# Two edits to a two-layer transformer kernel: modulation units summed on GpSimd, and a new order of the last expert group

## The reference

```python
cond = silu(c)                                   # (1, 1024)
mod = cond @ w_ada + b_ada                       # w_ada (1024, 6144), 24 MB
sh1, sc1, g1, sh2, sc2, g2 = split(mod, 6)
h = rms_norm(x) * (1 + sc1) + sh1
proj = h @ w_in                                  # hgrn2 branch, window attention, two gates
x = x + g1 * (merged @ w_out)
h2 = rms_norm(x) * (1 + sc2) + sh2
x = x + g2 * moe_ffn(h2, ...)                    # 32 experts, top 4, 12 MB of weights each
# second layer: stick-breaking attention, short convolution, then
y = y + einsum('nef,efd->nd', act, w_down[group])   # 32 experts of width 256, top 2
```

## Time and profile before

| | us |
|---|---|
| median of three runs | 1562.67 (1560.21 to 1562.7) |
| the profiled execution | 1558.39 |
| its span, first to last instruction | 1556.6 |
| prologue | 0 to about 235 |
| first mixture of experts | to about 1151 |
| second layer, mixing | to about 1341 |
| second mixture of experts | to the end |

### The profile page before, as it was taken

One profiled execution on the slowest core, in us unless ns is written; L12 is line 12 of the kernel. 1 busy time (PEld: TensorE's weight loads), 2 busy tenths in 40 slices (PEclk: granted clock), 3 DMA queues, 4 the chain that ended last, 5 costly groups with the idle time before them and its releaser, 6 DMA issues.

```text
span 1556.6 us, 20914 instructions
## 1 busy us (share of the span) xinstructions
PE 1451.0 (93%) x8700; PEld 757.0 (49%) x8700; DVE 602.3 (39%) x920; ACT 342.8 (22%) x395; POOL 22.7 (1%) x36
## 2 busy tenths in 40 slices
PE   5999999999999999998998989999989999997677
PEld 2878985333323333332332333333338999853343
DVE  3786683232213132321322321323247697422111
ACT  3564332010101010100100100101033474321110
POOL 1100100000000000000000000000000000000000
PEclk9999999999999999999999999999999999999889
DMA  9987589999999999999999999999996447999998
GB/s 382 367 324 276 198 353 398 428 429 429 429 428 425 428 429 428 429 428 427 429 428 428 428 427 429 428 427 428 428 403 218 163 163 287 364 385 423 422 422 316
DMA packets 76832, 594.63 MB, mean 382 GB/s; under 512 B 5434, under 2 KB 6688, under 8 KB 37348
## 3 DMA queue, kind: packets, MB, share of 16 engines
q1 hardware_dynamic: 74448, 588.25, 91.6%
q0 software_dynamic: 1792, 4.86, 0.9%
q10 hardware_dynamic: 532, 0.64, 0.1%
HBM read 592.66 MB, written 1.06 MB: 381 GB/s over the span
## 4 chain that ended last, share of the span: by engine, by line
PE 60%; DMA 35%; DVE 4%; issue 1%; ACT 1%; SPq 0%; DVEq 0%; ACTq 0%
PE PS L563 53%; DMA ring<-in_w_up 26%; DMA ring<-in_w_up_e 7%; PE PS L739 3%; DMA ring<-in_w_ada 1%; PE PS L1514 1%; DVE ring_r L361 1%; PE PS L763 1%; DVE arena L838 1%; PE PS L679 1%; ACT ring_r L356 0%; PE PS L1591 0%; DVE arena L2110 0%; DVE ring_r L1996 0%; DVE small L2101 0%
## 5 line engine op out<-in xcount | busy, mean ns | idle before, releaser
L563 PE MATMUL PS<-ring,arena 128*64 128x512 f32 x3020 | 670.7, 596 | 39.4 <-DMA ring<-in_w_up 27.2
L563 PEld LDWEIGHTS PS<-ring,arena 128*64 128x64 f32 x3020 | 212.4, 137 | 460.0 <-issue 400.7
L563 PE MATMUL PS<-arena 128*128 128x128 f32 (+12 forms) x1240 | 228.9, 441 | 3.7 <-ACT arena L559 1.4
L826 DVE TENSOR_SCALAR arena<-PS 128x512 f32<-128x512 f32 x32 | 22.1, 692 | 480.6 <-PE PS L563 480.6
L542 ACT ACTIVATE arena<-arena 128x512 f32<-128x512 f32 x32 | 20.2, 630 | 696.5 <-DVE arena L826 696.5
L563 PE MATMUL PS<-ring_r 128*128 128x256 f32 (+1 forms) x576 | 170.9, 304 | 0.4 <-DVE ring_r L1996 0.4
L563 PEld LDWEIGHTS PS<-arena 64*128 64x128 f32 (+6 forms) x1240 | 108.6, 164 | 121.3 <-issue 114.7
L563 PE MATMUL PS<-hT_r,ring_r 128*128 128x256 f32 x800 | 150.3, 284 | 0.4 <-DVE ring_r L361 0.4
L361 DVE TENSOR_TENSOR ring_r<-ring,ring_r 128x2048 fp32r<-128x2048 f32 x51 | 116.4, 2291 | 34.9 <-ACT ring_r L356 33.8
L563 PEld LDWEIGHTS PS<-hT_r,ring_r 128*128 128x128 f32 x800 | 126.6, 192 | 2.3 <-issue 1.4
L356 ACT ACTIVATE ring_r<-ring 128x2048 fp32r<-128x2048 f32 x51 | 97.2, 1912 | 102.5 <-PE PS L563 98.5
(11 more groups left out here) (382 smaller groups left out, 974.1 us busy)
## 6 DMA issues: line engine op xcount, KB each, us to landing
ring<-in_w_up SPq DMA_DIRECT2D x128, 2048.0 KB, 21.0
ring<-in_w_down SPq DMA_DIRECT2D x59, 2048.0 KB, 18.8
ring<-in_w_in SPq DMA_DIRECT2D x17, 2048.0 KB, 11.5
ring<-in_w_gate_e SPq DMA_DIRECT2D x14, 2048.0 KB, 19.3
ring<-in_w_down_e SPq DMA_DIRECT2D x13, 2048.0 KB, 20.9
ring<-in_w_up_e SPq DMA_DIRECT2D x13, 2048.0 KB, 19.4
ring<-in_w_ada SPq DMA_DIRECT2D x12, 2048.0 KB, 15.8
ring<-in_w_out SPq DMA_DIRECT2D x4, 2048.0 KB, 7.8
```

Of the source, the lines that this page charges most:

```text
L563: return nc.tensor.matmul(o, w, m, start=first, stop=last)
L826: V.tensor_scalar(glu.rearrange("p (kk b q) -> p kk b q", kk=4, b=2), hu[:, :, :, :, 0], 7.0, None, ALU.min)\
```

## The change

In the prologue six of the eight later modulation units (4, 6, 8, 9, 10, 11) are summed first. GpSimd, in place, multiplies each of the unit's two row blocks (128x2048) by its column of `cond` and adds the second to the first. TensorE then multiplies the one sum by a matrix of ones: 4 matmuls in place of 8. A sum starts when its unit has landed; TensorE waits for the sum. In TensorE's stream the units move back: 4 between the two halves of round 2, 6 behind the q and k transposes, beside 7, 8 behind round 5, 9 behind round 6, 10 behind the attention output, 11 behind round 7. The router loads in GpSimd's queue stand between the sums, and three bias loads count to `ffn_params` (so the counts that wait for it grow by three). Two semaphores are joined into `rowsT`.

In the last group the down weights come in twelve pieces: first the even rows of all columns (4 pieces), then the odd rows of the left columns, then of the right ones. TensorE multiplies both halves' even rows, then waits for `last_left`, finishes the left half, scatters its first tile, waits for `last_right`, finishes the right half, and scatters the other three tiles. Of the keep-warm matmuls, the six before the up matmuls become four, and the two before the down matmuls go.

```diff
+        ADA_SUMMED = (4, 6, 8, 9, 10, 11)
...
+        def moe2_scatter_tile(pe, X, it, b, i):
+            pe.wait_ge(S(f"{X}_ye"), 2 * it + b + 1)
+            mm(PS[:, 4 + 2 * b + i, :], swT2[:, i * P:(i + 1) * P], ye2[:, b * 512:(b + 1) * 512], True, True)\
+                .then_inc(S(f"{X}_scat_done" if i else f"{X}_scat_tile"), 1)
...
-                    keep_warm(6, 7)
+                    keep_warm(4, 7)
...
-            if last:
-                keep_warm(2, 7)
             arrived(pe, 4)
             arrived(pe, 5)
-            for b in range(2):
-                if by_columns and b:
-                    pe.wait_ge(S("last_columns"), 64)
-                for kk in range(2):
...
-                if by_columns:
-                    moe2_scatter(pe, X, it, b, True)
+            if by_columns:
+                down(0, 0)
+                down(1, 0)
+                pe.wait_ge(S("last_left"), 64)
+                down(0, 1)
+                moe2_scatter_tile(pe, X, it, 0, 0)
+                pe.wait_ge(S("last_right"), 64)
+                down(1, 1)
+                moe2_scatter_tile(pe, X, it, 0, 1)
+                for i in range(TT):
+                    moe2_scatter_tile(pe, X, it, 1, i)
...
-            for b in range(2):
+            for kk, c, name in ((0, slice(0, 1024), None), (1, slice(0, 512), "last_left"), (1, slice(512, 1024), "last_right")):
                 for i in (4, 5):
                     for o in range(2):
...
+            def ada_sum(n):
+                u, seen = ADA[n], 3 * ADA_SUMMED.index(n)
+                kp = PRE[u][2]
+                w = slots[SLOT_OF[u]].rearrange("p (k n) -> p k n", k=2)
+                wait(pool, loaded(u))
+                for kk in range(2):
+                    k = 2 * kp + kk
+                    nc.gpsimd.tensor_scalar(w[:, kk, :], w[:, kk, :], sm("cond")[:, k:k + 1], None, ALU.mult)\
+                        .then_inc(S("ada_summed"), 1)
+                pool.wait_ge(S("ada_summed"), seen + 2)
+                nc.gpsimd.tensor_tensor(w[:, 0, :], w[:, 0, :], w[:, 1, :], ALU.add).then_inc(S("ada_summed"), 1)
+            pool.wait_ge(S("cond32"), 1)
+            ada_sum(4)
+            small_load(sm("b_r1"), bc(t["b_router"][0]), "ffn_params")
...
+            router_load(0, 0)
+            ada_sum(6)
+            router_load(1, 0)
...
             pool.wait_ge(S("modrow"), 2)
             row_out(1)
+            for n, which, half in ((8, 2, 0), (9, 0, 1), (10, 1, 1), (11, 2, 1)):
+                ada_sum(n)
+                router_load(which, half)
...
-                for kk in range(2):
+                for kk in range(1 if summed else 2):
                     k = 2 * kp + kk
                     for j in range(4):
                         last = nc.tensor.matmul(PS[32 * j:32 * j + 32, 7, :],
-                                                sm("cond32")[:, 32 * k:32 * k + 32], w[:, kk, 512 * j:512 * (j + 1)],
...
+                                                C("ones")[:, 0:32] if summed else sm("cond32")[:, 32 * k:32 * k + 32],
+                                                w[:, kk, 512 * j:512 * (j + 1)],
...
             first_tokens()
-            ada(4)
...
             keep_warm_short(6, 4)
-            split_cols(2)
+            pe.wait_ge(S("consts"), 16)
+            split_cols(2, between=lambda: ada(4))
             ada(5)
-            ada(6)
             split_cols(3)
...
+            ada(6)
             ada(7)
             split_tokens(4)
...
-            pe.wait_ge(S("modrow"), 2)
-            ada(8)
...
             split_tokens(5)
+            pe.wait_ge(S("modrow"), 2)
+            ada(8)
+            split_cols(6)
             ada(9)
-            split_cols(6)
-            ada(10)
...
-            ada(11)
...
+            ada(10)
             pe.wait_ge(S("hg_scores_in"), 1)
...
             split_cols(7)
+            ada(11)
```

More of the change, by code:

```diff
@@ L752, in moe2_pe, with down @@
                 pe.wait_ge(S(f"{X}_xg"), 2 * it + 4)
-            if last:
-                keep_warm(2, 7)
             arrived(pe, 4)
             arrived(pe, 5)
-            for b in range(2):
-                if by_columns and b:
-                    pe.wait_ge(S("last_columns"), 64)
-                for kk in range(2):
[L761 to L766, removed]
-                if by_columns:
-                    moe2_scatter(pe, X, it, b, True)
+            def down(b, kk):
+                for j in range(4):
+                    q = slice(CAP2 * j, CAP2 * (j + 1))
+                    mm_ = nc.tensor.matmul(PS[q, b, :], aT2[:, kk * P + CAP2 * j:kk * P + CAP2 * (j + 1)],
+                                           moe2_dst(where, 4 + j // 2)[:, 2 * (j % 2) + kk, b * 512:(b + 1) * 512],
+                                           start=kk == 0, stop=kk == 1, tile_position=(0, CAP2 * j))
+                if kk:
+                    mm_.then_inc(S(f"{X}_down_done"), 1)
+            if by_columns:
[9 more added lines that the diff above has]
+                    moe2_scatter_tile(pe, X, it, 1, i)
+            else:
+                for b in range(2):
+                    for kk in range(2):
+                        down(b, kk)
             if not by_columns:
@@ L1156, in _ @@
             small_load(at(A2MAP, "gain"), bc(t["norm_ffn_g_2"][0]), "ffn_gain")
-        NSMALLS = 9 * 16
+        NSMALLS = 6 * 16
         lb_rows = t["lower_bound_logits"].rearrange("l (h k) -> (l h) k", k=P)
@@ L1508, in ada @@
                 b, kp = PRE[u][1:]
-                wait(pe, loaded(u))
                 w = slots[SLOT_OF[u]].rearrange("p (k n) -> p k n", k=2)
-                for kk in range(2):
+                summed = n in ADA_SUMMED
+                if summed:
+                    pe.wait_ge(S("ada_summed"), 3 * ADA_SUMMED.index(n) + 3)
+                else:
+                    wait(pe, loaded(u))
+                for kk in range(1 if summed else 2):
                     k = 2 * kp + kk
@@ L1514, in ada @@
                         last = nc.tensor.matmul(PS[32 * j:32 * j + 32, 7, :],
-                                                sm("cond32")[:, 32 * k:32 * k + 32], w[:, kk, 512 * j:512 * (j + 1)],
-                                                start=k == 0, stop=k == KD - 1, tile_position=(0, 32 * j))
+                                                C("ones")[:, 0:32] if summed else sm("cond32")[:, 32 * k:32 * k + 32],
+                                                w[:, kk, 512 * j:512 * (j + 1)],
+                                                start=k == 0, stop=kp == 3 and (summed or kk == 1), tile_position=(0, 32 * j))
                 last.then_inc(S("ada_done"), 1)
@@ L1525, in _ @@
             pe.wait_ge(S("posf"), 1)
-            nc.tensor.transpose(PS[:, 5, 0:2], rows[64:66, :], ident[64:66, 64:66]).then_inc(S("posT"), 1)
+            nc.tensor.transpose(PS[:, 5, 0:2], rows[64:66, :], ident[64:66, 64:66]).then_inc(S("rowsT"), 1)
             transpose_h(pe, "n1")
@@ L1533, in _ @@
                 last = nc.tensor.transpose(PS[:, 4, c * P:(c + 1) * P], modrow[:, 0, c * P:(c + 1) * P], ident)
-            last.then_inc(S("mod1"), 1)
+            last.then_inc(S("rowsT"), 1)
             keep_warm_short(6, 7)
             first_tokens()
-            ada(4)
             pe.wait_ge(S("hT_V"), 1)
@@ L2240, in _ @@
             sig(TV(bdown, bdown, G2[0:NE, :], ALU.mult), "bdown_scaled")
-            v.wait_ge(S("ffn_params"), 16 * 7)
+            v.wait_ge(S("ffn_params"), 16 * 10)
             v.wait_ge(S("row_in"), 64)
@@ L2372, in _ @@
             count["x_ready"] += 1
-            v.wait_ge(S("ffn_params"), 16 * 8)
+            v.wait_ge(S("ffn_params"), 16 * 11)
             ss, rs = sm("ss"), sm("rs")
```

30 lines of the change are left out of this document (13 added, 17 removed).

## The result

The changed kernel takes 1606.72 us (median of four runs, 1602.25 to 1607.9) against 1561.66 us for the kernel before beside it (1560.21 to 1562.7): a ratio of 1.0286, interval 1.0271 to 1.030, 45 us slower. The forecast was 1562.3, its range 1556.5 to 1576.5. The profiled execution took 1606.95 us, its span is 1604.7 us, 48.1 more than before.

The account below looks back on a forecast made before the run. It took VectorE's chain to set the prologue from 85.19 to 113.11, TensorE behind 115.56, and DMA the first mixture, passing prologue changes on whole. Prologue +1.3 and last group -1.7 gave -0.4: 1562.67 to 1562.3 us, range 1556.5 to 1576.5.

Parts of the forecast that it names:

- GpSimd's sums: Prologue: a sum takes 9.0 us (8.3 to 13.7); all are hidden except unit 10's, which stalls TensorE 2.2 us.
- unit 10: Prologue, behind the attention output: its sum is done at 136.6, wanted at 134.4; TensorE stands 2.2 us (1.5 to 6.9).
- a rival with a chance of 0.25: Prologue: GpSimd and VectorE hold each other up over SBUF reads; +16 there, +13.6 in all, 1576 us; chance 0.25.
- Late load of the projection unit: Prologue, ahead of 85 us: `w_in` 4 lands 2.7 us late, putting VectorE's chain at +0.8 us (-1.6 to +1.4).
- Unit 8 leaves the scores: Prologue, between two score groups: moving unit 8 away removes VectorE's 0.72 us wait at 100.27, gaining 0.7 us.
- Units behind 115.56: Prologue, after round 6 starts on TensorE: three units of 0.92 us replace two of 1.85, gaining 1.0 us in full.
- The last group: Kernel's end: the new order saves 2.6 us and the clock costs 0.9, together -1.7 us.
- its term: Last group, final up matmuls: idle after four keep-warm matmuls may lower the clock; 0 to 1.7 us, taken as 0.9.
- the weights: Last group: down weights are loaded by about 1545.4 and wanted at 1546.3, so covered by 0.9 us.
- The gap of 2.7 us: Last group: TensorE's idle time between the four keep-warm matmuls and the last up matmuls.
- a way to be wrong: Last group: a late load in the last eight pieces of down weights makes the last quarter wait.

Follow-up runs that it names:

- e8: The changed kernel with GpSimd's sums for units 10 and 11 alone, TensorE multiplying both row blocks of the other units: 1578.48 us, ratio 1.0112.
- e4: The changed kernel with GpSimd's scalings and addition on 8 of 2048 columns, all waits and orders kept: 1563.08 us, ratio 1.0013.
- e3: The changed kernel without GpSimd's sums, TensorE multiplying both row blocks of all units at the new places: 1570.75 us, ratio 1.0058.
- e5: The changed kernel with eight GpSimd memsets, which write and don't read, in place of each sum: 1577.02 us, ratio 1.0104.
- e7: e4 with five keep-warm matmuls in TensorE's wait between the score groups, where unit 8 stood before: ratio 1.0015.
- e10: e3 with unit 8 back between the score groups, the other units at their new places: 1566.36 us, ratio 1.0037.
- e9: The changed kernel with eleven keep-warm matmuls ahead of unit 10, in TensorE's wait for GpSimd's sum: ratio 1.0256.

## Why the prediction was wrong

**The step that failed** is *GpSimd's sums*. It failed in two ways.

*The length.* I took a scaling at 2.2 us, near the memset, and the addition's 4.55 as the upper bound, since a scaling has one input less. It takes 5.43 us, more than the addition beside it (4.7 to 4.9), so a sum is 16 us, outside the 8.3 to 13.7. Unit 6's sum, which I called hidden, made TensorE wait 5.18 us, which VectorE's lateness covered. In the forecast the length decides unit 10: its load, the last in a late row of loads, landed 13.5 us behind its issue as predicted (144.97 to 158.4), and the wait for the sum is 11.25 us where I had 2.2 and at most 6.9. e8 shows 8.9 for this alone.

*The sharing.* It was a rival with a chance of 0.25, and it is what happened: e4 and e3 against the changed kernel show that 36 to 43 us of the 45 go with GpSimd's time, and the rows show the holds themselves. SBUF — State Buffer in the Trainium skill, under Who interferes with whom, states these cases: two SBUF inputs against a GpSimd that reads, and a TENSOR_SCALAR in a two-port mode against any; reads of PSUM and reductions go free. The trace agrees on the kinds (2.3 to 4.3 us; 5.24 and 9.92; none at 119.44 and at L2141). It also says that the other side blocks for the whole instruction. That the trace doesn't bear out in two ways: beside GpSimd's scalings VectorE's two-input instructions got through with a third of the scaling still to run, and the split at 185.55 wasn't held at all; in e5 the hold ran over several memsets in a row, 10 us of 14. I argued from the absence of a row, where nothing spoke against the rule. I sized the rival at +16: 7 + 4.5 + 4.5. With sums of 16 us and a chain of holds it is 29.2, of which 25.7 stand at round 6 (29.1 less the 3.4 of the order). I had also let its lateness shrink the stall of unit 10 to 1 us; TensorE's order brings that unit's load later with everything else, so it didn't shrink.

**The terms of the prologue, by e4.**
- Late load of the projection unit: the mechanism was right, the size 1.6 where I said 0.8 (the load took 14 us from issue, not 13.3, in the changed kernel 61.30 to 75.35).
- Unit 8 leaves the scores: -0.7 predicted, +1.8 measured. I saw the wait of 0.72 us behind it, not the one of 0.62 us at 102.32, and not that the unit filled TensorE's own wait for VectorE. Without it TensorE stood 5.49 us and the clock fell. e7 gives the clock back and with it 2.0 us at the split; e10, which puts the unit back, has 1.13 us for the first score group alone, and the split only 0.2 us earlier than e3's.
- Units behind 115.56: -1.0 predicted, nothing measured in e4 (+3.4 at the split, +3.5 at the branch's end): the saving of 0.8 us (three units of 0.96 for two of 1.85) is taken by the 0.73 us wait for ScalarE's copy that unit 11 had covered.
- The clock in the prologue had no term. It cost 2.0 us in the small matmuls behind unit 10's wait, 0.9 in unit 10 itself, and part of the 2.1 us by which the stretch up to unit 11 is longer than in e4.

**The last group:** -1.7 predicted, -2.0 measured, partly by luck: the clock came out 0.9 us better than its term, the weights 0.5 us worse. The clock cost nothing (the pass at 1586.80 took 3.66 us; the pass ahead had run long at the low clock, so that the four keep-warm matmuls ended only 0.96 us before it). The weights were not covered: TensorE waited 0.52 us for the left pieces. The gap of 2.7 us that I expected stands in ten of the other traces, with the clock lost in three, so the cost does come and go as the term supposed; e4's 1.88 us wait is the late load that I had named as a way to be wrong.

The end of the sum: +3.5 by the order, 25.7 by the holds, 16.3 by unit 10 (11.25 of wait, 2.0 in the small matmuls, the rest in round 7 and its neighbours, partly at the lower clock), -2.0 at the end, are 43.5, and with the 4.8 us that appear in the first mixture 48.3, against 48.1 between the spans.

## What to carry to other kernels

An idle GpSimd is not free beside a busy VectorE: look which of VectorE's instructions will run at that time and where their inputs are, and price each with two inputs in SBUF as held for up to one GpSimd instruction that reads. A hold moves all that follows, and with it which instructions the next one meets, so a half dose can cost much less than half. Before you move an operation off a slow place, look whether it was filling a wait: here TensorE stood 5.49 us without it, and its clock fell. A missing row for the new operation deserves a run of one instruction before it deserves an estimate.

## What the runs showed of the hardware

- A GpSimd TENSOR_SCALAR of 128x2048 with a scalar for each partition takes 5.43 us (2.65 ns an element), of 128x1024 2.83; an addition of 128x2048 with two inputs 4.7 to 4.9, and 5.96 beside a split of VectorE that had begun first; a memset 1.75.
- VectorE rows of 0.25 to 2.3 us with two inputs in SBUF grew by up to 4.30 us beside a GpSimd that reads. Beside an addition they got through at its end, beside a scaling of 5.4 to 5.7 us mostly 3.6 to 3.9 us after it began, and one that began 3.9 us into a scaling wasn't held.
- A VectorE TENSOR_SCALAR of 128x768 was held 5.24 us beside a scaling, to its end. One of 128x16 waited 9.9 us beside back-to-back memsets of 1.75 us, without getting in between two of them, while reductions and TENSOR_TENSOR beside the same memsets kept their 2.28 and 0.17 us.
- The time that TensorE stands idle doesn't settle the clock by itself here: behind the same four keep-warm matmuls and 2.6 to 2.7 us of idle it was at 2.4 GHz through the next pass in seven traces (3.66 us) and lower in three (5.0 to 5.2 us). In e9's trace 9.7 us of keep-warm matmuls ahead of 2.05 us of idle didn't keep it. In e3 and e7 it fell with TensorE busy.
